# RMS and layer-norm statistics on one core: squares as the stationary operand, one mean column streamed

## What is computed

```
rmsnorm(x, g):      x * rsqrt(mean(x*x) + 1e-6) * g
layernorm(x, g, b): (x - mean) * rsqrt(var + eps) * g + b
layer 0: x = x + g * rmsnorm(conv_module(modulated rmsnorm(x)));  x = x + g * rmsnorm(swiglu(modulated rmsnorm(x)))
layer 1: the same with attention in place of the convolution
conv_module: product, gate, convolution of 31 taps, layernorm over channels, silu, product
second model, two layers: layernorm(a*x + token_mixing(x)), then layernorm(a*x + conv_ffn(x))
```

## Time and profile before

| | |
|---|---|
| median of 3 runs | 1968.42 us (1966.68 to 1971.39) |
| span of the profiled execution | 1969.0 us |
| PE busy | 1889.2 us, 96% |
| PEld busy | 1668.6 us, 85% |
| DVE busy | 1201.8 us, 61% |
| ACT busy | 953.6 us, 48% |
| POOL busy | 542.5 us, 28% |

### The profile page before, as it was taken

The page is one execution under the profiler, slowest core; times in us unless marked ns, Lnnn a source line. Parts: engine busy times, 40 slices in busy tenths (PEclk is TensorE's granted clock), DMA queues, the critical chain, the costliest instruction groups (busy, mean ns, idle before and its releaser), DMA issues.

```text
span 1969.0 us, 36121 instructions
## 1 busy us (share of the span) xinstructions
PE 1889.2 (96%) x14718; PEld 1668.6 (85%) x14718; DVE 1201.8 (61%) x2440; ACT 953.6 (48%) x1709; POOL 542.5 (28%) x685
## 2 busy tenths in 40 slices
PE   6999999999998989999998999999999999999998
PEld 4855778888886857899987989999999899989997
DVE  4989763233338575655579675685648876567473
ACT  4314532232224477544456474565555556456464
POOL 1320010000001533000021222747373322374736
PEclk9999999999999999899999999999999999999999
DMA  9335442222224254655544444455554544545551
GB/s 358 128 108 206 151 150 96 97 97 97 97 97 171 86 193 175 211 182 182 183 160 175 142 136 160 165 168 172 194 182 152 174 148 133 168 150 178 187 178 59
DMA packets 84548, 307.24 MB, mean 156 GB/s; under 512 B 9376, under 2 KB 10656, under 8 KB 84128
## 3 DMA queue, kind: packets, MB, share of 16 engines
q1 hardware_dynamic: 84384, 304.94, 45.4%
HBM read 303.86 MB, written 1.05 MB: 155 GB/s over the span
## 4 chain that ended last, share of the span: by engine, by line
PE 82%; DVE 10%; ACT 5%; DMA 2%; issue 1%; SPq 0%; POOL 0%; DVEq 0%; ACTq 0%
PE pb L540 18%; PE pb L542 18%; PE pb L541 18%; PE pb L513 7%; PE pb L514 6%; PE pb L519 6%; DVE wlo L1897 2%; DMA raw<-wstream 2%; ACT whi L1237 1%; PE pb L591 1%; DVE Y L2146 1%; PE pb L765 1%; PE pb L924 1%; PE pb L1108 1%; PE pb L1121 1%
## 5 line engine op out<-in xcount | busy, mean ns | idle before, releaser
L540 PE MATMUL pb<-Hh,whi 128*128 128x256 f32 (+1 forms) x2304 | 701.8, 305 | 1.8 <-DVE SM L2480 1.6
L542 PE MATMUL pb<-Hh,wlo 128*128 128x256 f32 (+1 forms) x2304 | 694.6, 301 | 0.0
L541 PE MATMUL pb<-Hl,whi 128*128 128x256 f32 (+1 forms) x2304 | 694.6, 301 | 0.0
L1237 ACT ACTIVATE whi<-raw 128x1024 fp32r<-128x1024 f32 x468 | 489.3, 1054 | 318.1 <-PE pb L542 171.2
L2855 POOL TENSOR_TENSOR wlo<-raw,whi 128x256 fp32r<-128x256 f32 x576 | 434.9, 790 | 734.9 <-ACT whi L1237 733.9
L1897 DVE TENSOR_TENSOR wlo<-raw,whi 128x1024 fp32r<-128x1024 f32 x324 | 421.2, 1305 | 344.1 <-ACT whi L1237 343.7
L540 PEld LDWEIGHTS pb<-Hh,whi 128*128 128x128 f32 x2304 | 441.9, 192 | 22.9 <-DVE SM L2480 2.5
L541 PEld LDWEIGHTS pb<-Hl,whi 128*128 128x128 f32 x2304 | 442.2, 192 | 15.0
L542 PEld LDWEIGHTS pb<-Hh,wlo 128*128 128x128 f32 x2304 | 442.0, 192 | 15.0
L513 PE MATMUL pb<-Hh,whi 128*128 128x256 f32 (+1 forms) x528 | 161.2, 327 | 4.6 <-ACT Hh L1311 3.2
L514 PE MATMUL pb<-Hh,wlo 128*128 128x256 f32 (+1 forms) x528 | 158.8, 322 | 0.0
(11 more groups left out here) (333 smaller groups left out, 2952.6 us busy)
## 6 DMA issues: line engine op xcount, KB each, us to landing
raw<-wstream SPq DMA_DIRECT2D x572, 512.0 KB, 3.5
X<-xin SPq DMA_DIRECT2D x2, 1024.0 KB, 7.7
out<-X SPq DMA_DIRECT2D x8, 128.0 KB, 1.8
CON<-consts SPq DMA_DIRECT2D x1, 926.0 KB, 8.6
VEC<-vecs SPq DMA_DIRECT2D x1, 662.0 KB, 9.5
CON<-consts SPq DMA_DIRECT2D x1, 147.0 KB, 3.8
VEC<-vecs SPq DMA_DIRECT2D x1, 88.0 KB, 2.0
```

The lines of the kernel that those rows point to most:

```text
L540: e.matmul(dst, hi, xh, start=k == 0, stop=False)
L541: e.matmul(dst, hi, xl, start=False, stop=False)
L542: i = e.matmul(dst, lo, xh, start=False, stop=k == kt - 1)
L1237: e.activation(whi[:, s % NPIECE, :], raw[:, p % NRAW, :], ACT.Copy).then_inc(sig("act_hi", ("hi", p)), 1)
```

## The change

Every statistic of the norms named above is made with the tile as stationary operand and one column of 1/1024 streamed, so that the tokens come out on the partitions: column c holds tokens 128 c to 128 c + 127. Four columns hold 512 tokens and two hold 256, and the square roots, reciprocals and the operations of `residual_norm` and of the convolution's norm work on these. `widen` broadcasts a column as the stationary operand and streams the identity, once for each 128 tokens. The constant `quad` is gone, and `XM` has 4 columns instead of 128. Which calls there are, and where they stand, is as before.

```diff
-            def quarters(S, tile, n, start, stop, point):
-                b = slots.at(("stat", S))
-                for c in range(4):
-                    i = e.matmul(b[32 * c:32 * c + 32, 0:n // 4], con("mean", 0, 32), tile[:, c * n // 4:(c + 1) * n // 4],
-                                 start=start, stop=stop)
+            def columns(b, o, tile, n, start, stop, point):
+                for c in range(n // 128):
+                    i = e.matmul(b[:, o + c:o + c + 1], tile[:, c * 128:(c + 1) * 128], con("mean", 0, 1),
+                                 start=start and c == 0, stop=stop and c == n // 128 - 1)
                 i.then_inc(sig("pe_stat", point), 1)
...
-                for key, o in ((S + "b", 128), (S + "c", 256)):
+                for key, o in ((S + "b", 4), (S + "c", 8)):
                     w.wait_ge(*on("acc", key))
...
+                    columns(b, o, slots.at(("acc", key)), 512, False, False, ("asum", key))
...
             def widen(S, n, *until, ring="pt", r=None, idle=0):
...
-                r = slots.at(("root", S))[:, 0:n // 4] if r is None else r
+                r = slots.at(("root", S)) if r is None else r
                 w.wait_ge(*on("rec", S))
-                for c in range(4):
-                    i = e.matmul(b[:, c * n // 4:(c + 1) * n // 4], con("quad", c, c + 1).broadcast_to((128, 128)), r,
+                for c in range(n // 128):
+                    i = e.matmul(b[:, c * 128:(c + 1) * 128], r[:, c:c + 1].broadcast_to((128, 128)), con("ident"),
                                  start=True, stop=True)
...
-                            token_sums(b, 0, t, first and m == 4, last and m == 7, ("csum", l, F, m))
+                            columns(b, 0, t, T, first and m == 4, last and m == 7, ("csum", l, F, m))
...
-                e.activation(t[:, 0:128], slots.at(("stat", S))[:, 0:128], ACT.Sqrt, bias=con("eps6")).then_inc(
+                e.activation(t[:, 0:4], slots.at(("stat", S))[:, 0:4], ACT.Sqrt, bias=con("eps6")).then_inc(
...
-                t = slots.at(("root", S))[:, 0:n // 4]
+                t = slots.at(("root", S))[:, 0:n // 128]
                 w.wait_ge(*on("root", S))
                 e.reciprocal(t, t).then_inc(sig("dve_rec", ("rec", S)), 1)
...
-                step(e.tensor_tensor(q, b[:, 256:384], ry, ALU.mult))
+                step(e.tensor_tensor(q, b[:, 8:12], ry, ALU.mult))
                 after()
-                step(e.scalar_tensor_tensor(out=q, in0=b[:, 128:256], scalar=2.0, in1=q, op0=ALU.mult, op1=ALU.add), ("fresh", R))
+                step(e.scalar_tensor_tensor(out=q, in0=b[:, 4:8], scalar=2.0, in1=q, op0=ALU.mult, op1=ALU.add), ("fresh", R))
```

More of the change, by code:

```diff
@@ L281, in build @@
         SM = sb("SM", [128, 256])
-        XM = sb("XM", [128, 128])
+        XM = sb("XM", [128, 4])
         csz = sb("csz", [128, 8, 32 + 2 * (MOST - 1)])
@@ L625, in sums, with token_sums @@
                 i.then_inc(sig("pe_stat", point), 1)
-            def quarters(S, tile, n, start, stop, point):
-                b = slots.at(("stat", S))
-                for c in range(4):
-                    i = e.matmul(b[32 * c:32 * c + 32, 0:n // 4], con("mean", 0, 32), tile[:, c * n // 4:(c + 1) * n // 4],
-                                 start=start, stop=stop)
+            def columns(b, o, tile, n, start, stop, point):
+                for c in range(n // 128):
+                    i = e.matmul(b[:, o + c:o + c + 1], tile[:, c * 128:(c + 1) * 128], con("mean", 0, 1),
+                                 start=start and c == 0, stop=stop and c == n // 128 - 1)
                 i.then_inc(sig("pe_stat", point), 1)
+            def token_sums(S, tile, n, start, stop, point):
+                columns(slots.at(("stat", S)), 0, tile, n, start, stop, point)
             def sums3(S, R, step):
@@ L642, in sums3 @@
                 b = slots.at(("stat", S))
-                for key, o in ((S + "b", 128), (S + "c", 256)):
+                for key, o in ((S + "b", 4), (S + "c", 8)):
                     w.wait_ge(*on("acc", key))
-                    for c in range(4):
-                        i = e.matmul(b[32 * c:32 * c + 32, o:o + 128], con("mean", 0, 32),
-                                     slots.at(("acc", key))[:, c * 128:(c + 1) * 128], start=False, stop=False)
-                    i.then_inc(sig("pe_stat", ("asum", key)), 1)
+                    columns(b, o, slots.at(("acc", key)), 512, False, False, ("asum", key))
                 for k in (6, 7):
                     step()
-                    for key, o in ((S, 0), (S + "b", 128), (S + "c", 256)):
+                    for key, o in ((S, 0), (S + "b", 4), (S + "c", 8)):
                         w.wait_ge(*on("sq", key, k))
[L653 to L657, removed]
+                        columns(b, o, slots.at(("sq", key, k)), 512, False, o == 8 and k == 7,
+                                ("sums", key) if k == 7 else ("xsum", key, k))
                 step()
@@ L666, in sums_y @@
                 tile = slots.at(("acc", S) if k is None else ("sq", S, k))
[L667 to L670, removed]
+                columns(b, 0, tile, 512, not k, False, ("asum", S) if k is None else ("xsum", S, k))
             def acc_sums(S, n, until=None):
@@ L707, in x_sums @@
                     w.wait_ge(*on("sq", R, k))
-                    quarters(R, slots.at(("sq", R, k)), n, k == 0, k == 7, ("sums", R) if k == 7 else ("xsum", R, k))
+                    token_sums(R, slots.at(("sq", R, k)), n, k == 0, k == 7, ("sums", R) if k == 7 else ("xsum", R, k))
                     if k in own:
@@ L747, in norm_sums @@
                 w.wait_ge(*on("fin", k))
-                quarters("cz", Y[:, k * 512:(k + 1) * 512], 512, first, last, ("zsum", k))
+                token_sums("cz", Y[:, k * 512:(k + 1) * 512], 512, first, last, ("zsum", k))
                 w.wait_ge(*on("sq", "cv", k))
-                quarters("cv", slots.at(("sq", "cv", k)), 512, first, last, ("sums", "cv") if last else ("xsum", "cv", k))
+                token_sums("cv", slots.at(("sq", "cv", k)), 512, first, last, ("sums", "cv") if last else ("xsum", "cv", k))
             w.wait_ge(*on("pad"))
@@ L776, in tensor @@
                     w.wait_ge(*on("cv", 0))
-                    quarters("cs", Y[:, 0:512], 512, True, False, ("zsum", "cs"))
+                    token_sums("cs", Y[:, 0:512], 512, True, False, ("zsum", "cs"))
                     w.wait_ge(*on("cv", 1))
-                    quarters("cs", Y[:, 512:1024], 512, False, True, ("sums", "cs"))
+                    token_sums("cs", Y[:, 512:1024], 512, False, True, ("sums", "cs"))
                 if i_ == 13:
@@ L798, in tensor @@
             r = slots.at(("root", "cv"))
-            widen("cv", 512, ("ctm", 7), r=r[:, 0:128], idle=2)
-            widen("cvm", 512, ("ct", 7), r=r[:, 128:256])
+            widen("cv", 512, ("ctm", 7), r=r[:, 0:4], idle=2)
+            widen("cvm", 512, ("ct", 7), r=r[:, 4:8])
             bite(2)
@@ L1202, in centered @@
                     db = bank("pt", ("dmean", l, F), ("lessd", l, F, 7), ("lnd2", l, F))
-                    token_sums(db, T, ds, True, True, ("lnds", l, F))
+                    columns(db, T, ds, T, True, True, ("lnds", l, F))
                     squares((7,), last=True)
```

41 lines of the change are left out of this document (17 added, 24 removed).

## The result

The changed kernel takes 2034.24 us (median of 4 runs, 2030.96 to 2038.19) beside 1969.91 us for the kernel before on the same chip: a ratio of 1.032, with an interval of 1.030 to 1.0339, or 63 us (59 to 67). The forecast was 2003 us and its range ended at 2017; the sign and the mechanism were right, the size was not.

The account below looks back on a forecast made before the run. The prediction took TensorE, busy 96% of the span, as the bound. To 1969 us it added 17.7 us at unchanged clock and 16 us for the falling clock, giving 2003 us, range 1983 to 2017.

Parts of the forecast that it names:

- x0, y0, y1: First norm and two big 512-token norms: +1.0, +4.3 and +6 us at unchanged clock; falling clock +1, +5 and +4.
- convolution: Convolution's norm up to the next layer's first matmul: +5 us at unchanged clock, and +5 more for the falling clock.
- y2, r2, y3: Three 256-token norms: smaller reciprocals and cheaper widening outweigh the dearer last call, about -0.5 us each, -1.6 together.
- layer norms: Four centered layer norms: +0.8 us each, +3.0 together at unchanged clock, and +1 for the clock.
- The price of a call: A TensorE sum call goes from 0.275 to 0.91 us for 512 tokens, from 0.14 to 0.46 for 256.
- The small operations: Operations behind the sums shrink to 4 or 2 columns: each reciprocal saves 0.75 or 0.35 us, others about 0.1.
- the credit of 1.2: At the layer after the convolution, some half clock behind a DMA wait may go: +5 us taken instead of +6.2.
- The clock: Long stretches of narrow records in the big norms let TensorE's clock fall to half: +16 us in all.
- rival A: Same sums with the clock kept throughout: +17.7 us, 1987 us, from 1981 to 1993; chance 0.33.
- The price of a narrow record at half clock: Taken from eight records of a widen: 0.178 us each at half clock against 0.114, so 0.065 more.
- How much lies in the stretch: Half the records after the convolution pay, +5 us with dense work; y0 +5; y1 +4, partly behind DMAs.
- rival D: The clock also falls beside the layer norms and at tap 24, some 2 us each: 2013 to 2025; chance 0.12.

Follow-up runs that it names:

- experiment 1: The changed kernel with wider streams of the same mean matrix (40 columns in x0, y0, y1, 128 elsewhere) instead of one column: 1993.96 us, ratio 1.0113 to the kernel before.
- experiment 7: The kernel before with only the three 256-token norms y2, r2 and y3 in the new form, 128 columns streamed: 1973.25 us, ratio 1.000.
- Experiment 10: The kernel before with only the convolution's norms in the new form, 128 columns streamed instead of one: 1978.34 us, ratio 1.0045.
- experiment 12: The kernel before, unchanged, run and profiled a second time: 1970.06 us, ratio 0.9996.
- experiments 2, 6 and 9: Changed kernel with the convolution's norms old again, 2007.75 us; kernel before with only x0, y0, y1 new, one column, 1998.59 us; the same with 40 columns, 1982.25 us.
- X: The group x0, y0, y1 and what follows from them; new alone in the kernel before, one column streamed: 1998.59 us, ratio 1.0129.
- C: The group of the convolution's norms; put back to the old form in the changed kernel: 2007.75 us, ratio 1.0187 to the kernel before.
- experiment 6: The kernel before with only x0, y0, y1 and the roots and residual norms behind them new, one column streamed: 1998.59 us, ratio 1.0129.

## Why the prediction was wrong, point by point

The table sets the sum beside the runs. "Wide" is the price with a wide stream, "narrow less wide" what one column adds.

| part | predicted, clock unchanged | measured, wide | predicted, clock | measured, narrow less wide |
|---|---|---|---|---|
| x0, y0, y1 | 1.0 + 4.3 + 6 = 11.3 | 13 (9 to 17) | 10 | 12 |
| convolution | 5 | 9 (6 to 11) | 5 | 11 |
| y2, r2, y3 | -1.6 | 0 (-2 to +2) | 0 | 3 |
| layer norms | 3.0 | 0 to 5 (by lags, see below) | 1 | 1 to 6 |
| all | 17.7 | 22 (18 to 26) | 16 | 41 |

The layer norms were not run alone with a wide stream. By the lags of experiment 1 they cost 4.8 us against the first profile of the kernel before and 0.1 against the second, so their row is rough.

- **The price of a call: right.** 0.89 to 0.92 us for 512 tokens; a block of five calls for 256 between two projections adds 1.3 to 1.4 us of lag, predicted 1.6. The load sets the pace, whatever is streamed. The estimate from the Trainium skill ("TensorE: Matmul & The Clock Gate", LDWEIGHTS) in the prediction, 0.85 us, is 4 to 8% under it at full clock; at half clock a call takes 1.71 us, for which that section has no figure.
- **The small operations: right in size, and worth nothing**, as it was said for y0: reciprocals 0.95 to 0.18 us, hidden behind TensorE's queue. For y2, r2 and y3, where the sum saw a gain of 1.6, experiment 7 shows none.
- **The sum without the clock: 17.7 against 22 (some 30 at an equal clock, by the estimate behind experiment 1), mainly in the convolution.** Experiment 10 started 0.8 us late. Without that, its first scaling moves from 177.79 to 189.19 by 10.6 us (9.5 predicted), and the next layer by 7.5, so that the wait for the DMA absorbed 3.1 (3.3 predicted): these steps held. What failed is the profile that the stage was set against. Its half clock cost it 3.4 us and was not the kernel's but that execution's (experiment 12); beside the second profile the stage costs 8.9 us, as the measured 9 says, and the credit of 1.2 did not exist.
- **The clock: 16 against 41 (some 33 over the kernel before, by the same estimate). This is the step that failed.** The mechanism was right (rival A, the clock kept, is out by the page of the kernel after, and experiment 1 shows the narrow stream as the cause), the size was not, for four reasons.
 - *The price of a narrow record at half clock.* I took 0.178 us from eight widening records from 1478.23 to 1479.65. The clock falls inside this very row. Stretches of the kernel before:

```profile
1478.20:1478.60 0.40, 0.37 (x4) 0.40 (x4) 0.40 (x2) 0.38 (x2) 0.07 (x1) 0.98 0.73 297
1478.60:1479.00 0.40, 0.40 (x4) 0.40 (x4) 0.40 (x2) 0.40 (x1) 0.40 (x1) 0.50 0.94 379
1479.00:1479.60 0.60, 0.60 (x5) 0.60 (x5) 0.02 (x1) 0.60 (x1) 0.60 (x2) 0.50 0.86 335
```

   The records start at 1478.23, .37, .48, .59, .80, 1479.01, .23 and .44: the first three ran at full clock and the other five are 0.21 us apart. The true price is 0.217 us: 0.104 more than at full clock instead of 0.065.
 - *How much lies in the stretch.* Behind the convolution I let half of the records pay, 3.2 us. All 64 of the last eight calls do: 8 x (1.71 - 0.90) = 6.5 us. The 160 tap records after tap 24 add 8.05 - 5.53 = 2.5, the fourth call there 0.6, bite and warm-up about 1.5: some 11 instead of 5, and the lags of experiment 1 and of the kernel after differ by 11 in this stage. At y0 the step was nearly right: 1.0 + 2.5 for the blocks, 1.7 for two bites and 0.9 for the warm-up are 6.1, against 5. At y1 two blocks (5.0), four bites (3.5) and a widening (0.9) are 9.4, against 4: I had hidden part of it behind full DMA rings, and nothing of it hid: the bites of y1 wait 0.74, 1.37 and 0.42 us for DMAs in the kernel before, but in experiment 1 and in the kernel after these waits are gone, since the loads alone use them up.
 - *The stages that I left out.* Taps and the 256-token norms stood in rival D only, which had a chance of 0.12. The kernel after has half clock beside r2 (842 to 856; 4.6 us lost there against experiment 1), where the kernel before has it too (796 to 806), but for a shorter time.
 - *The second model.* Half clock stands at 1125 to 1133, 1600 to 1607, 1811 to 1819 and 1821 to 1829 in the kernel after, the first ahead of all four layer norms; the kernel before has shorter ones, from 1479 to 1482 and from 1547 to 1550. Against experiment 1 the lag grows by 8 us from 856 us to the end. The prediction had +1.
- **What its last part named** was seen: narrow records at 0.11 us, TensorE without idle time from the taps to the twelfth call, reciprocals under 0.2 us, half clock near 183, 255 and 651. It missed the bound on how much of the narrow work the fall would catch: at the upper end all of it, with the dense work behind it. Had every narrow record behind the taps, in y0 and in y1 been priced at 0.217 us (240 x 0.104 = 25) and eight bites and warm-ups at 0.9 us more (7), the upper bound of this term would have been 32 us or more, and the range would have reached 2020 and beyond.

Open: the parts alone sum to 54 or 55 us and the whole is 63 (59 to 67). With a wide stream the three parts that were run sum to 22 without the layer norms, and the whole is 22, within the intervals. In half-clock time, on the mean of all executions, the parts add 25 (convolution), 33 (x0, y0, y1), 14 (layer norms) and 5 us (y2, r2, y3), 77 together; the whole adds 84 to 89.

Two pieces of the missing 8 us are seen in the traces. One is y1 (15.5 against 11.9 us). The other lies outside the norms and at full clock. In three stretches of dense projections between y0 and y1 (336 to 382, 455 to 497 and 570 to 597 us of the kernel before) the matmul records start 0.233 us apart in the kernel before and in the kernel after, and 0.227 us apart in experiments 2, 6 and 9, the three with X new and C old. The same length of time in one such stretch, first in the kernel before, then in experiment 6:

```profile
332.00:384.00 52.00, 52.00 (x225) 42.08 (x224) 14.23 (x13) 14.91 (x20) 0.00 (x0) 1.00 0.27 91
...
343.00:395.00 52.00, 52.00 (x231) 43.07 (x230) 14.24 (x13) 16.03 (x21) 0.00 (x0) 1.00 0.27 91
```

TensorE is busy all the time and the clock is full in both, and yet more records pass. This gives those three kernels 3.1 us that the kernel after doesn't get, so that X alone looks cheaper than it is in the whole, and undoing C alone seems to give back more. Why the spacing differs was not tried. What brings the fall at y1 forward was not tried either.

No version beats the kernel before. The one part without a loss gains nothing.

The Trainium skill ("TensorE: Matmul & The Clock Gate", HAM oscillation — how this bites in real kernels) tells of a clock that falls in idle gaps while TensorE waits for DMAs. In the first profile of the kernel before a wait of 2.66 us lies at the beginning of its stretch from 181 to 189. That fits in kind, though the waits in that section's example are 3 to 5 us long; the second profile, with 2.09 us, kept the clock. The falls of the kernel after don't fit: TensorE is busy 14.00 of 14 us at y0, and what differs from experiment 1 is only the number of columns streamed.

## What to carry to other kernels

Turning a reduction round so that the data are the stationary operand trades a cheap stream for a full load per 128 columns: 0.9 us for 0.275 here, and the operations it shrinks pay only if they stand on the path that ends last. Where the form must be used, stream a wide operand even if one column is wanted: 40 or 128 columns cost at most 5% of a call in these runs and kept the clock, worth 41 of 63 us (widths between 1 and 40 were not tried). Before a price "at half clock" is taken from a row, cut the row into short windows and see whether the clock fell inside it. And before a stretch at half clock is counted as the kernel's, profile the kernel a second time.

## What the runs showed of the hardware

- A stationary load of 128 float32 columns sets the pace of its matmul: 0.111 to 0.117 us a record with 1, 40 or 128 columns streamed at full clock, 0.217 us at half clock (one column). So the pace that the load sets slows down with the clock.
- Back-to-back matmuls of one column let the granted clock fall to half with TensorE busy all the time, and with bites of 512 columns between them it stayed there until the narrow work was over (255 to 269, 651 to 672).
- The same instructions can meet the fall a few microseconds earlier or later (y0: 11.5 or 13.1 us in two profiles of the kernel after), and a stretch at half clock behind a DMA wait was in one profile of the kernel before and not in the other.
- Dense float32 matmuls of 512 columns start 0.227 or 0.233 us apart at full clock with TensorE busy all the time, in the same stretch of the program, according to which norms ahead of it have the new form. No run shows why.
